# Attention heads started during the query projection, and an output projection cut into parts by pairs of heads

## The reference, cut to what matters

```python
def attn_mixer(h, w_qkv, q_norm, k_norm, w_out, cos, sin):
    proj = h @ w_qkv                        # 1024 -> 8 query, 2 key, 2 value heads of 128
    q, k, v = split(proj)
    q = apply_rope(rmsnorm(q, q_norm), cos, sin)
    k = apply_rope(rmsnorm(k, k_norm), cos, sin)
    # per query head, all 256 tokens, no mask; 4 query heads share a key and value head
    p = softmax(q @ k.T * 128 ** -0.5)
    o = p @ v
    return o @ w_out                        # 1024 -> 1024, added to x by the caller
```

## Time and profile before

| | |
|---|---|
| median of 3 runs | 1169.71 us (1164.8 to 1170.99) |
| the profiled execution | 1162.0 us |
| its span in the trace | 1160.2 us |
| mean granted TensorE clock | 0.984 of 2.4 GHz |
| TensorE, VectorE, ScalarE busy | 93%, 70%, 57% of the span |
| stretch of the attention layer | about 386 to 487 us |
| start of its feed-forward network's first sums | 487.6 us |

### The profile page before, as it was taken

How to read it: one execution, slowest core, us unless ns; L and a number is a source line. 1 busy time by engine, 2 the same in 40 slices (tenths; PEclk the granted TensorE clock), 3 DMA queues, 4 the chain that set the end, 5 groups by cost and what they waited for, 6 DMA issues and landing times.

```text
span 1160.2 us, 25926 instructions
## 1 busy us (share of the span) xinstructions
PE 1084.0 (93%) x10950; PEld 1013.6 (87%) x10950; DVE 811.3 (70%) x1329; ACT 659.6 (57%) x902; POOL 6.5 (1%) x15
## 2 busy tenths in 40 slices
PE   4999988999999987999999988899999999999997
PEld 3999888898989865889999988888889888789997
DVE  4963658757576566477776765598898889955573
ACT  5834546555555654456556554665666657666443
POOL 0000000000000000000000000000000000000000
PEclk9999999999999998989999998999999999999999
DMA  7543345676745331236555553433333233124541
GB/s 242 167 158 108 136 155 181 247 264 229 263 160 182 109 110 37 82 118 208 175 180 195 193 155 121 134 112 110 110 111 110 84 101 111 61 71 129 191 135 37
DMA packets 132990, 167.69 MB, mean 145 GB/s; under 512 B 2656, under 2 KB 124512, under 8 KB 131488
## 3 DMA queue, kind: packets, MB, share of 16 engines
q1 hardware_dynamic: 131632, 153.51, 40.7%
q0 software_dynamic: 1264, 12.78, 2.9%
HBM read 164.18 MB, written 2.10 MB: 143 GB/s over the span
## 4 chain that ended last, share of the span: by engine, by line
PE 79%; DVE 12%; ACT 5%; DMA 2%; issue 2%; SPq 0%; DVEq 0%; ACTq 0%
PE bank L312 17%; PE bank L313 15%; PE bank L314 15%; DVE wl L274 2%; PE banks L615 2%; PE banks L619 2%; PE banks L617 2%; PE bank L615 2%; PE bank L617 2%; PE bank L619 2%; DVE hf L2260 1%; ACT wh L269 1%; PE bank L652 1%; PE banks L1081 1%; PE bank L1113 1%
## 5 line engine op out<-in xcount | busy, mean ns | idle before, releaser
L312 PE MATMUL bank<-xh,wh 128*128 128x256 f32 x1376 | 404.8, 294 | 13.3 <-DVE xl L1811 5.9
L313 PE MATMUL bank<-xl,wh 128*128 128x256 f32 x1408 | 400.0, 284 | 0.0
L314 PE MATMUL bank<-xh,wl 128*128 128x256 f32 x1376 | 390.8, 284 | 0.0
L312 PEld LDWEIGHTS bank<-xh,wh 128*128 128x128 f32 x1376 | 265.1, 193 | 24.0 <-issue 13.1
L274 DVE TENSOR_TENSOR wl<-raw,wh 128x2048 fp32r<-128x2048 f32 x97 | 221.5, 2286 | 74.3 <-ACT wh L269 74.2
L313 PEld LDWEIGHTS bank<-xl,wh 128*128 128x128 f32 x1408 | 271.8, 193 | 0.8 <-issue 0.7
L314 PEld LDWEIGHTS bank<-xh,wl 128*128 128x128 f32 x1376 | 265.3, 193 | 0.0
L269 ACT ACTIVATE wh<-raw 128x2048 fp32r<-128x2048 f32 x97 | 184.7, 1907 | 69.0 <-PE bank L619 52.1
L298 DVE TENSOR_TENSOR wl<-raw,wh 128x1024 fp32r<-128x1024 f32 x86 | 103.7, 1218 | 22.9 <-ACT wh L290 22.8
L2260 DVE SCALAR_TENSOR_TENSOR hf<-big,vecs,hf 128x256 f32<-128x256 f32 x240 | 101.4, 478 | 0.0
L290 ACT ACTIVATE wh<-raw 128x1024 fp32r<-128x1024 f32 x86 | 87.6, 1057 | 8.9 <-PE bank L314 5.5
(11 more groups left out here) (390 smaller groups left out, 2219.2 us busy)
## 6 DMA issues: line engine op xcount, KB each, us to landing
raw<-in_ffn_w_up SPq DMA_DIRECT2D x44, 1024.0 KB, 5.1
raw<-in_w_in SPq DMA_DIRECT2D x36, 1024.0 KB, 5.4
raw<-in_ffn_w_down SPq DMA_DIRECT2D x22, 1024.0 KB, 5.0
raw<-in_gla_w_in SPq DMA_DIRECT2D x12, 1024.0 KB, 6.3
big<-in_ada_w POOLq DMA_DIRECT2D x8, 1536.0 KB, 8.7
raw<-in_attn_w_qkv SPq DMA_DIRECT2D x6, 1024.0 KB, 5.0
raw<-in_gla_w_out SPq DMA_DIRECT2D x4, 1024.0 KB, 5.1
raw<-in_attn_w_out SPq DMA_DIRECT2D x4, 1024.0 KB, 6.7
```

The costliest lines, as they stand in the source:

```text
L312: nc.tensor.matmul(ps, wh, xh, start=start, stop=False)
L313: nc.tensor.matmul(ps, wh, xl, start=False, stop=False)
L314: return nc.tensor.matmul(ps, wl, xh, start=False, stop=stop)
```

## The change

The PSUM banks and the order of the instructions on TensorE, ScalarE and VectorE in the attention layer are other ones. No arithmetic is added or removed: the same matmuls, activations and vector operations are issued, and each `qk_` helper takes one group where it took several.

- The heads' first steps stand among the last two blocks of queries: the scores of heads 0 and 1 follow the first half of block 4.
- The sums and turns of group e follow one group at a time, one half block later each.
- Sums and turns use the banks 3, 4, 5, 5, 5; the transposed probabilities use bank 7 alone, the heads' product bank 6, the modulation columns bank 3; the output projection uses the banks 1, 2, 0, 1.
- `out_part(j, pair)` takes two heads instead of four, 12 matmuls in each part. The parts stand in the head steps; the last pair's parts of blocks 0 to 2 and the whole of block 3 follow after the last head.
- `qk_sums` waits, from the fourth group on, for the rope of the group before (same bank); `turn_probs` waits for the copy of the head before; `out_part(j, 0)` waits until block 3 + j of the projection is copied out; the feed-forward network of this layer waits for two added blocks.

The core of the diff:

```diff
-    if N_AOUT <= n < N_F1:
-        return 5 + (n - N_AOUT) % RING
...
+        QK_BANK = (3, 4, 5, 5, 5)
...
-                if layer == 0:
-                    pe.wait_ge(out_added, 3)
+                pe.wait_ge(out_added, 6 if layer else 3)
...
+            def qk_sums(e):
+                pe.wait_ge(sem("qk_squares"), e + 1)
+                if e == 0:
+                    pe.wait_ge(sem("rstd_columns"), 1)
+                if e >= 3:
+                    pe.wait_ge(sem("qk_roped"), e)
+                nc.tensor.matmul(PS[QK_BANK[e]][:, :], ones, SQ10[:, 2 * e:2 * e + 2, :], start=True, stop=True)\
+                    .then_inc(sem("qk_square_sums"), 1)
...
             def turn_probs(h):
                 pe.wait_ge(sem("probs_ready"), h + 1)
-                if h >= 2:
-                    pe.wait_ge(sem("probs_t_taken"), h - 1)
+                if h:
+                    pe.wait_ge(sem("probs_t_taken"), h)
...
-                        last = nc.tensor.transpose(PS[1 + h % 2][:, st * T + tt * P:st * T + (tt + 1) * P],
+                        last = nc.tensor.transpose(PS[7][:, st * T + tt * P:st * T + (tt + 1) * P],
...
-                    last = nc.tensor.matmul(PS[0][:, 0:T], VA[:, st, (h // 4) * P:(h // 4 + 1) * P],
+                    last = nc.tensor.matmul(PS[6][:, 0:T], VA[:, st, (h // 4) * P:(h // 4 + 1) * P],
...
-            def out_part(j, half):
+            def out_part(j, pair):
                 n = N_AOUT + j
-                if half == 0:
+                if pair == 0:
                     pe.wait_ge(w_lo_ready, n + 1)
-                    if j == RING:
+                    if j < RING:
+                        pe.wait_ge(evacuated, E_QKV + 4 + j)
+                    else:
                         pe.wait_ge(out_added, 5)
-                for k in range(4 * half, 4 * half + 4):
+                pe.wait_ge(sem("attn_split"), 2 * pair + 2)
+                for k in (2 * pair, 2 * pair + 1):
...
+            half_of(1, 0)
+            qk_sums(0)
+            half_of(1, 1)
+            half_of(2, 0)
+            qk_turns(0)
+            half_of(2, 1)
+            half_of(3, 0)
+            qk_sums(1)
+            half_of(3, 1)
+            qk_turns(1)
+            half_of(4, 0)
+            qk_sums(2)
             attend_scores(0)
             attend_scores(1)
+            half_of(4, 1)
+            qk_turns(2)
+            turn_probs(0)
+            half_of(5, 0)
+            qk_sums(3)
+            attend_out(0)
+            attend_scores(2)
+            turn_probs(1)
+            half_of(5, 1)
+            qk_turns(3)
+            attend_out(1)
+            attend_scores(3)
+            turn_probs(2)
+            out_part(0, 0)
             qk_sums(4)
+            attend_out(2)
+            attend_scores(4)
+            turn_probs(3)
+            out_part(1, 0)
+            qk_turns(4)
+            attend_out(3)
+            attend_scores(5)
+            turn_probs(4)
+            out_part(2, 0)
+            out_part(0, 1)
+            attend_out(4)
+            attend_scores(6)
+            turn_probs(5)
+            out_part(1, 1)
+            attend_out(5)
+            attend_scores(7)
+            turn_probs(6)
+            out_part(2, 1)
+            out_part(0, 2)
+            attend_out(6)
+            turn_probs(7)
+            out_part(1, 2)
+            out_part(2, 2)
+            attend_out(7)
+            mod_turned()
+            for j in range(RING):
+                out_part(j, 3)
+            for pair in range(4):
+                out_part(RING, pair)
```

`half_of(j, m)` is one half (24 matmuls) of projection block j. ScalarE's and VectorE's new orders in the same stretch:

```diff
+            split_hi(act, N_QKV + 2)
+            qk_square(0)
+            split_hi(act, N_QKV + 3)
+            qk_rsqrt(0)
+            values_taken()
+            split_hi(act, N_QKV + 4)
+            queries_taken(1)
+            split_hi(act, N_QKV + 5)
+            qk_rsqrt(1)
+            queries_taken(2)
+            split_hi(act, N_AOUT)
+            qk_rsqrt(2)
+            exps(0)
+            exps(1)
+            turned_taken(0)
+            queries_taken(3)
+            split_hi(act, N_AOUT + 1)
+            qk_rsqrt(3)
+            out_hi(0)
+            exps(2)
+            turned_taken(1)
+            queries_taken(4)
+            out_hi(1)
+            exps(3)
+            turned_taken(2)
+            split_hi(act, N_AOUT + 2)
+            qk_rsqrt(4)
+            for h in range(4, QH):
+                out_hi(h - 2)
+                exps(h)
+                turned_taken(h - 1)
...
+            lo(N_QKV + 2)
+            lo(N_QKV + 3)
+            qk_norm(0)
+            lo(N_QKV + 4)
+            rope(0)
+            lo(N_QKV + 5)
+            qk_norm(1)
+            rope(1)
+            lo(N_AOUT)
+            qk_norm(2)
             negated_max(0)
             negated_max(1)
             normalise(0)
             rope(2)
+            normalise(1)
+            lo(N_AOUT + 1)
+            qk_norm(3)
+            negated_max(2)
+            out_lo(0)
+            normalise(2)
+            rope(3)
+            negated_max(3)
+            out_lo(1)
+            normalise(3)
+            lo(N_AOUT + 2)
+            qk_norm(4)
+            negated_max(4)
+            out_lo(2)
+            normalise(4)
+            rope(4)
+            for h in range(5, QH):
+                negated_max(h)
+                out_lo(h - 2)
                 normalise(h)
```

More of the change, by code:

```diff
@@ L838, in _ @@
[L838 to L853, removed]
@@ L902, in out_part, with mod_turned @@
                                                 skip_group_check=True)
-                if half:
+                if pair == 3:
                     last.then_inc(block_done, 1)
+            def mod_turned():
+                for h in range(2):
+                    rows = P - 64 * h
+                    for q in range(4):
+                        last = nc.tensor.matmul(PS[3][:, 16 * h + q:16 + 8 * h:4],
+                                                ada_rows[h][0:rows, q * P:(q + 1) * P], ident[0:rows, 0:rows:32],
+                                                start=True, stop=True)
+                last.then_inc(sem("mod_summed"), 1)
@@ new lines, in half_of @@
+            def half_of(j, m):
+                n = N_QKV + j
+                if m == 0:
+                    pe.wait_ge(w_lo_ready, n + 1)
+                    if j >= RING:
+                        pe.wait_ge(evacuated, E_QKV + j - RING + 1)
+                ms = slice(m * P, (m + 1) * P)
+                for k in range(KT):
+                    if j == 2 and m == 0:
+                        qk_ready(k)
+                    ps, s = PS[bank_of(n)][:, m * T:(m + 1) * T], n % RING
+                    if j == 1:
+                        eh, el = EARLY[2]
+                        last = three(ps, WH[:, s, k, :], WL[:, s, k, :], eh[:, k, ms], el[:, k, ms], k == 0, k == KT - 1,
+                                     True)
+                    else:
+                        last = three(ps, WH[:, s, k, ms], WL[:, s, k, ms], XH[:, k, :], XL[:, k, :], k == 0,
+                                     k == KT - 1)
+                if m:
+                    last.then_inc(block_done, 1)
@@ new lines, in _ @@
+            early_product(2, N_QKV, bank_of(N_QKV))
+            pe.wait_ge(sem("rstd_ready"), 3)
+            for tt in range(2):
+                last = nc.tensor.transpose(PS[3][:, T + tt * P:T + (tt + 1) * P], RS[:, tt * P:(tt + 1) * P], ident)
+            last.then_inc(sem("rstd_turned"), 1)
+            half_of(1, 0)
[6 more added lines that the diff above has]
+            qk_sums(1)
@@ L1507, in _, with qk_rsqrt @@
[L1507 to L1520, removed]
-                    take(n, j, E_QKV, QK[:, QK_AT[j - 1]:QK_AT[j - 1] + 2, :])
-                if j != 1:
-                    qk_square(max(j - 1, 0))
-                if j == 2:
-                    qk_rsqrt(0, 1)
-                if j == 4:
-                    qk_rsqrt(2, 3)
+            def qk_rsqrt(e):
+                act.wait_ge(sem("qk_square_sums"), e + 1)
+                rsqrt(SQ10[:, 2 * e:2 * e + 2, :], PS[QK_BANK[e]][:, :].rearrange("p (m t) -> p m t", m=2), 1.0 / P,
+                      eps_rms, "qk_rstd")
@@ new lines, in queries_taken, with values_taken @@
+            def queries_taken(e):
+                n = N_QKV + 1 + e
+                act.wait_ge(block_done, n + 1)
+                nc.scalar.activation(QK[:, QK_AT[e]:QK_AT[e] + 2, :],
+                                     PS[bank_of(n)][:, :].rearrange("p (m t) -> p m t", m=2), ACT.Copy)\
+                    .then_inc(evacuated, 1)
+                qk_square(e)
+            def values_taken():
+                n = N_QKV + 1
+                act.wait_ge(block_done, n + 1)
+                act.wait_ge(sem("rstd_columns"), 1)
+                act.wait_ge(evacuated, E_QKV + 1)
+                for tt in range(2):
+                    last = nc.scalar.activation(VA[:, tt, :], PS[bank_of(n)][:, tt * T:(tt + 1) * T], ACT.Identity,
```

(2 more changed lines are left out.)

116 lines of the change are left out of this document (25 added, 91 removed).

## The result

The changed kernel took 1152.1 us in the median of four executions (1151.8 to 1154.9), the kernel before 1167.4 on the same chip: a ratio of 0.987 with a 95% interval of 0.984 to 0.991, 1.3% faster. In a second comparison, six executions against 23, the medians were 1154.1 and 1165.8, the ratio 0.989 (0.986 to 0.991). The forecast was 1158.9, with a range from 1153.0: the direction was right, the gain larger than forecast (15.3 and 11.8 us in the medians, against 10.8). The first median lies 0.9 us under the range, the second inside it.

What follows compares the result with a forecast made beforehand. Bound: the heads' chain of small steps, leaving TensorE idle or slow-clocked. Gaps falling from 17.4 to 10.0 us gain 7.4, the clock 3.4, together 10.8: from 1169.7 to 1158.9 us, range 1153.0 to 1166.5.

Steps and rivals of the forecast that it cites:

- The count of TensorE's work and the gaps: Attention layer: 85.4 us of TensorE work at full clock stays; gaps fall from 17.4 to 10.0 us, gaining 7.4.
- rival 3: Transposes wait for the previous head's copy out of single bank 7: 5.3 us come back, gain 5.5, 1164.2; chance 0.10.
- Rival 4: Heads don't run beside the projection; late links in in-order queues return 7.2 us, gain 0.2, 1169.5; chance 0.08.
- The clock: Slow stretches behind TensorE's gaps in the attention layer: loss falls from 7.1 to 3.7 us, gaining 3.4.
- The step that took one slow stretch behind the long gap and one behind a short one: Of six new gaps, the 3.3 us one and one of 0.8 to 1.6 drop the clock, losing 3.7 us.
- From the profile to the median: Whole kernel: the 10.8 us gain, a difference within one stretch, comes off the median 1169.7, leaving 1158.9.
- No drop of the clock: Rival: the new order's gaps in the attention layer cost no clock; gain 14.5 us, 1155.2; chance 0.20.
- As many drops as before: Rival: five or six slow stretches behind the gaps, 9 to 11 us; gain 3.5 to 5.5, 1165; chance 0.12.
- no effect: Rival: heads slip behind late queue links and the clock loses 7.1 us as before; gain 0.2, 1169.5; chance 0.08.
- a clock that stays low through the mixed stretch: Rival: from 392 to 470 us the clock stays low; for 40 us, 5.5 us slower, 1175; chance 0.05.
- The first wait: Sums of group 0, within the values' block: TensorE waits 3.3 us for ScalarE's squares instead of 2.13, 1.2 worse.
- The wait before output block 3: End of the output projection: TensorE newly waits 1.6 us for VectorE's cut to free block 3's ring slot.

Runs made afterwards that it cites:

- the order with the moved sums: The changed kernel with group 0's sums and turns one half block later on TensorE: stretch 107.12 and 107.10 us, ratios to before 0.987 and 0.988.
- the filled gaps: Extra unused matmuls in the head gaps of the kernel before: stretch 117.95 us, ratio 0.996; 24 in the changed kernel's 3.2 us gap: 108.19 us, 0.986.
- the early heads without the parts: The changed kernel, but with the output projection in halves of four heads as before: stretch 115.1 us, ratio to before 0.991.

## Why the prediction was wrong, point by point

**The count of TensorE's work and the gaps (right).** The gaps were forecast as 10.0 us and are 9.4; the gain from them was forecast as 7.4 and is 7.9. Each gap is within 0.3 us of its forecast. (The named gaps of before add up to 17.25, not 17.4.) The cost of the new waits for banks was put at nothing, and no transposes wait for the copy out of the single bank 7: rival 3 is out. By the Trainium skill's rule on rotating banks ("Perfetto Trace Analysis", section "Matmuls"), which wants the emptying of one bank to overlap the next group's matmuls, giving the rotation up should have cost something; here no wait shows. Two sets of transposes start 4.2 us or more apart, and each 0.6 us copy ends 1.5 us or more before the next set. Rival 4 is out by the same rows.

**The clock (right in kind, mis-sized).** The step that took one slow stretch behind the long gap and one behind a short one was half wrong: the first came, in all four profiles (of three kernels) that have the gap of 3.2 us, the second didn't come in either profile of the changed kernel. The clock's part of the gain was forecast as 3.4 us and is 12.2 - 7.9 = 4.3. With the gaps' 0.5 this makes 12.2 in the stretch instead of 10.8. Both terms of the 3.4 were too large. TensorE is busy for 96.5 us in the stretch when its clock is 1.00 throughout (the order with the moved sums), for 102.4 before and 98.05 in the changed kernel: 5.9 us were lost and not 7.1, and 1.6 are and not 3.7. The 7.1 was what the count of work left over, and the 85.4 us of that count were about 1.4 too few. That the slow clock is a cost of its own and not hidden behind ScalarE and VectorE is shown by the filled gaps: 4.0 us in the kernel before, 1.6 in the changed one.

**From the profile to the median (this step failed).** The prediction said that the gain is a difference within one stretch and took it off 1169.7. Two things were wrong with that step. The median of three executions was no good base: with a fourth it is 1167.4, in the comparison with 23 executions 1165.8, and they fall in clusters at 1162, 1165 and 1170. And the profile, at 1162.0, was of the lowest cluster: it is not 7.7 us of constant offset under the median but an execution in which less clock was lost, 3.4 us of it in this very stretch in the one profile taken of the highest cluster. The gap of 3.55 us that "cost no clock" there costs it in that one. So the order of before loses more in some executions than its profile showed, while the stretch of the changed kernel was 109.7 in both of its profiles. Of the 6.8 us between the forecast 1158.9 and the measured 1152.1, then, 2.3 are the base (1169.7 against 1167.4), 1.4 are the stretch (12.2 against 10.8), and about 0.9 the longer stretch of the highest cluster, if its seven executions are alike. The cause of the last 2.2 us stays open. They lie within the spread of the executions (1164.8 to 1171.0, and 1151.8 to 1154.9), and the second comparison, whose gain is 11.8 us, doesn't have them; that the range was missed by 0.9 us in one comparison and met in the other can't be told from chance.

**The rivals.** No drop of the clock (14.5) and the forecast (10.8) enclose what the stretch shows. As many drops as before, no effect, and a clock that stays low through the mixed stretch did not happen: from 406.9 to 466.3 us it was 1.00.

**The moved sums (right).** The first wait was called worse by 1.2 us, and it is by 1.07; putting the sums back gives that and the clock behind it, 2.6 us together. The wait before output block 3 was called 1.6 and is 1.5, but it was not all to be had: when 0.9 us of it went, the wait for the next network's preparation grew by 0.5, and the clock fell behind that.

## What to carry to other kernels

Where a chain of small steps over several engines leaves TensorE idle, start it under the last blocks of the matmuls before it, and then fill what is left with pieces of the next projection: pieces alone fill nothing while no input is finished. Lay the in-order queues out with measured durations; for the changed kernel it gave six gaps within 0.3 us and named a misplaced step worth 1.1 us of waiting and, as it turned out, 2.6 in all. (For the early heads without the parts it was off by up to 1.2 us at one gap.) Judge an edit of some microseconds by the stretch it changes, in several profiles, and count the clock behind a gap as its own term: a shorter sum of gaps can cost more if one of them grows.

## What the runs showed of the hardware

- The time to reach the attention layer, in code that no variant changes, was 386.2 to 391.7 us over fourteen profiles of nine kernels, and the part behind the stretch took 651.8 to 653.5. The time of whole executions goes with their mean granted clock (0.983 to 0.984, 0.981 to 0.983, and 0.979 in the three clusters of before).
- Whether the clock falls behind a gap did not go by its length alone. Over these profiles it fell behind the gap of 3.2 us before the first sums in 4 of 4, behind 3.55 in 2 of 5, behind 2.13 in 1 of 9, behind 1.98 before the next network's third pair in 6 of 8, and behind 1.48 at that same place in none of 6. Behind the 1.79 ahead of the stretch it fell in 13 of 14, and in the early heads without the parts it fell once 2.5 us after a gap of only 0.69. What TensorE did before differs: a whole block of dense matmuls ahead of the 2.13, two pairs with sums ahead of the 1.98. But that can't be all, since one kernel has the same gap behind the same work and the clock falls in one execution and not in another (2.13, 3.55 and 1.98 in the four profiles of before). What decides it was not tested. The Trainium skill ("TensorE: Matmul & The Clock Gate", section "What's actually happening") says that how busy TensorE has been recently sets the clock. The filled gaps agree with it in kind: with matmuls in them no slow piece came behind them.
- Extra matmuls made a kernel faster: 84 of them in the gaps of the kernel before took 4.0 us off its stretch.
